# Head scores by blocks of 32 and 64, and reordered steps at the group changes of a hybrid Fourier / HGRN2 diffusion step

## The reference, cut to what matters

```python
def trunk_layer(x, cond, w_mod, b_mod, norm_pre, norm_post, ffn_w_in, ffn_w_out, ...):
    mod = (jax.nn.silu(cond) @ w_mod + b_mod)[:, None, :]
    sh1, sc1, g1, sh2, sc2, g2, sh3, sc3, g3 = jnp.split(mod, N_MOD, axis=-1)
    h = rms_norm(x, norm_pre[0]) * (1.0 + sc1) + sh1
    x = x + 0.5 * g1 * rms_norm(swiglu(h, ffn_w_in[0], ffn_w_out[0]), norm_post[0])
    h = rms_norm(x, norm_pre[1]) * (1.0 + sc2) + sh2
    m, s_f, s_b = mixer(h, w_in, w_four, hgrn_gain, w_hgrn, w_out, lb, s0_f, s0_b, rows)
    x = x + g2 * rms_norm(m, norm_post[1])
    h = rms_norm(x, norm_pre[2]) * (1.0 + sc3) + sh3
    x = x + 0.5 * g3 * rms_norm(swiglu(h, ffn_w_in[1], ffn_w_out[1]), norm_post[2])
```

## Time and profile before

| what | value |
|---|---|
| median of 3 runs | 1507.5 (1505.93 to 1507.74) |
| profiled execution, its own time | 1505.78 |
| its span | 1504.0 |
| PE busy | 1455.7 (97%), 9059 matmul instructions |
| PEld busy | 1342.7 (89%) |
| DVE, ACT, POOL busy | 423.7, 485.4, 615.1 |
| DMA, share of 16 engines (queue q1) | 36.3% |
| mean granted TensorE clock | 0.994 |

### The profile page before, as it was taken

How to read it: one execution, slowest core, us unless ns; L and a number is a source line. 1 busy time by engine, 2 the same in 40 slices (tenths; PEclk the granted TensorE clock), 3 DMA queues, 4 the chain that set the end, 5 groups by cost and what they waited for, 6 DMA issues and landing times.

```text
span 1504.0 us, 21142 instructions
## 1 busy us (share of the span) xinstructions
PE 1455.7 (97%) x9059; PEld 1342.7 (89%) x9059; DVE 423.7 (28%) x616; ACT 485.4 (32%) x666; POOL 615.1 (41%) x486
## 2 busy tenths in 40 slices
PE   3999999999999999999999999999999999999997
PEld 2889989999887878999999999988999999998876
DVE  3311111211001431387777322135211111110042
ACT  5312122222233553233443322266212222232233
POOL 1333333344566663232222334543223343356664
PEclk9999999999999999999999999999999999999999
DMA  9576554222545551211111222323122222235454
GB/s 324 184 234 215 182 190 160 71 83 73 164 128 154 166 205 43 60 46 46 50 50 47 71 71 84 122 75 85 43 71 71 71 85 71 71 103 160 129 183 167
DMA packets 215137, 173.19 MB, mean 115 GB/s; under 512 B 6456, under 2 KB 175620, under 8 KB 214916
## 3 DMA queue, kind: packets, MB, share of 16 engines
q1 hardware_dynamic: 212676, 170.78, 36.3%
q10 hardware_dynamic: 2368, 1.07, 0.2%
HBM read 168.65 MB, written 3.17 MB: 114 GB/s over the span
## 4 chain that ended last, share of the span: by engine, by line
PE 90%; DVE 4%; ACT 3%; issue 1%; POOL 1%; DMA 1%; SPq 0%; DVEq 0%; ACTq 0%
PE PP L496 59%; PE PP L515 7%; PE PP L517 7%; PE PP L516 7%; PE PP L793 2%; PE PP L554 2%; PE PP L690 1%; PE PP L540 1%; DVE XTOK L1483 1%; POOL W_lo L461 1%; DMA W_in<-in_ffn_w_out 1%; DVE YB L1471 1%; DVE W_lo L1509 1%; PE PP L809 1%; ACT W_hi L998 0%
## 5 line engine op out<-in xcount | busy, mean ns | idle before, releaser
L461 POOL TENSOR_TENSOR W_lo<-W_in,W_hi 128x512 fp32r<-128x512 f32 (+1 forms) x452 | 575.0, 1297 | 873.6 <-ACT W_hi L998 873.2
L998 ACT ACTIVATE W_hi<-W_in 128x1024 fp32r<-128x1024 f32 x217 | 229.4, 1058 | 672.4 <-PE PP L496 468.9
L496 PE MATMUL PP<-Hhi,W_hi 128*128 128x320 f32 (+1 forms) x1792 | 417.8, 312 | 0.0
L496 PE MATMUL PP<-Hhi,W_lo 128*128 128x320 f32 (+1 forms) x1792 | 412.0, 309 | 0.0
L496 PE MATMUL PP<-Hlo,W_hi 128*128 128x320 f32 (+1 forms) x1792 | 411.9, 309 | 0.0
L496 PEld LDWEIGHTS PP<-Hhi,W_hi 128*128 128x128 f32 x1792 | 299.1, 188 | 12.9 <-issue 12.7
L496 PEld LDWEIGHTS PP<-Hlo,W_hi 128*128 128x128 f32 x1792 | 300.9, 188 | 0.0
L496 PEld LDWEIGHTS PP<-Hhi,W_lo 128*128 128x128 f32 x1792 | 300.5, 188 | 0.0
L515 PE MATMUL PP<-W_hi,Mhi 128*128 128x512 f32 x440 | 173.3, 394 | 6.8 <-DVE W_lo L1509 4.9
L517 PE MATMUL PP<-W_hi,Mlo 128*128 128x512 f32 x440 | 171.9, 391 | 0.0
L516 PE MATMUL PP<-W_lo,Mhi 128*128 128x512 f32 x440 | 171.9, 391 | 0.0
(11 more groups left out here) (213 smaller groups left out, 1367.6 us busy)
## 6 DMA issues: line engine op xcount, KB each, us to landing
W_in<-in_ffn_w_out SPq DMA_DIRECT2D x176, 256.0 KB, 3.4
W_in<-in_ffn_w_in SPq DMA_DIRECT2D x83, 512.0 KB, 3.8
modl<-in_w_mod SPq DMA_DIRECT2D x14, 2048.0 KB, 9.5
W_in<-in_w_in SPq DMA_DIRECT2D x32, 512.0 KB, 3.8
modw<-in_w_mod SPq DMA_DIRECT2D x4, 2048.0 KB, 13.8
HL<-g_rows SPq DMA_DIRECT2D x6, 512.0 KB, 5.9
V_in<-in_w_in SPq DMA_DIRECT2D x10, 256.0 KB, 5.1
O_in<-in_w_out SPq DMA_DIRECT2D x10, 256.0 KB, 5.5
```

The costliest lines, as they stand in the source:

```text
L461: return nc.gpsimd.tensor_tensor(lo[:, k0:k1, :], full[:, k0:k1, :], hi[:, k0:k1, :].bitcast(fp32), ALU.subtract)
L496: m = mm(out[:, 0:c1 - c0], w[:, k, :], src[:, c0:c1], start=lead and n == 0 and a == 0, stop=tail and n == len(x) - 1 and a == 2)
L998: A(W[i][0], W[i][2], ACT.Copy).then_inc(hi_done, 1)
```

## The change

1. **Head scores.** The diagonal and levels 1 to 6 are made in blocks of 32 x 32 (20 matmuls of 32 columns in place of 5 of 128; for each tile four, one on each 32-column group of the array), level 7 in blocks of 64 x 64 (10 matmuls). Levels 1 to 5 are merged under a mask of 32 columns into a small tile `ATN`; level 6 copies `ATN` and its own blocks into `AT` with eight copies, level 7 with two.
2. **Start.** GpSimd takes (2, 0) third and waits before it until four k slices of the first tokens are ready; ScalarE makes the second high part before the modulation row.
3. **First output, second group.** VectorE makes slab 3's low part between the gains of block 0 and block 1, and slab 20's goes to GpSimd. The first slabs of the value stage alternate between kept buffers and the ring, with other release points.
4. **Mixer's output.** ScalarE takes tile 3's second square and `y_std` before tile 2's `h_high_half`, which comes before `x_square` of tile 3; `h_hi` of tile 2 comes after `x_hat` of tile 3. VectorE follows.
5. **Second output.** Slab 3's low part is moved as in 3. The last three slabs run by token tile (`last_slabs`), tile 3 first; the last tile's add and store are made in two halves.

```diff
-    ("vuA", 8, [1, 2, 0] + KEEP, False), ("vuB", 8, [1, 2, 0] + KEEP, True),
+    ("vuA", 8, [6, 1, 7, 2, 8, 0, 9, 10], False), ("vuB", 8, [6, 1, 7, 2, 8, 0, 9, 10], True),
...
-    for n, k in enumerate((11, 14, 17, 21, 21)):
-        free[base["vuA"] + 3 + n] = base["out0B"] + half + k // 2
+    for n, k in ((0, 11), (2, 14), (4, 17), (6, 21), (7, 21)):
+        free[base["vuA"] + n] = base["out0B"] + half + k // 2
...
-    FIRST_LO = [(0, 0), (1, 0), (0, 1), (1, 1), (2, 0), (2, 1)]
-    LO_DVE = [BASE["out0B"] + m for m in (3, 7, 10, 13, 17, 20)]
+    FIRST_LO = [(0, 0), (1, 0), (2, 0), (0, 1), (1, 1), (2, 1)]
+    LO_DVE = [BASE["out0B"] + m for m in (3, 7, 10, 13, 17)]
...
+            if (i, half) == (2, 0):
+                pool.wait_ge(sem("h0_ready"), KT // 2)
...
+        def last_slabs():
+
+            n = out_slabs(2)
+            for t in GROUP[1]:
+                for m in range(2 * n - LAST, 2 * n):
+                    wide(BASE["out1B"] + m, Mhi, Mlo, 2 * (m % n), (t,), lambda t: y_bank(2, t, 1), False,
+                         m == 2 * n - 1, "y_done" if t == 3 else None, t == 4)
...
             for ch in range(NCH):
-                cols = tile_cols(ch)
-                m = mm(flat(pair_of(hd, 0))[:, cols], KX[0][:, cols], QD[:, 0, hd % 2, cols], start=True, stop=True)
+                for q in range(4):
+                    at = ch * P + 32 * q
+                    m = mm(near(pair_of(hd, 0))[32 * q:32 * q + 32, ch, :], KX[0][:, at:at + 32],
+                           QD[:, 0, hd % 2, at:at + 32], start=True, stop=True)
...
-                m = mm(flat(pair_of(hd, lev))[:, tile_cols(ch)], KX[lev % 2][:, tile_cols(ch)],
-                       level_ap(QD, hd, ch * P, P, 1 << (lev - 1)), start=True, stop=True)
+                if lev == 7:
+                    for q in range(2):
+                        at, other = ch * P + 64 * q, ch * P + 64 * (1 - q)
+                        m = mm(far(pair_of(hd, lev))[64 * q:64 * q + 64, ch, :], KX[lev % 2][:, at:at + 64],
+                               QD[:, 1 - q, hd % 2, other:other + 64], start=True, stop=True)
+                    continue
+                for q in range(4):
+                    at, other = ch * P + 32 * q, ch * P + 32 * (q ^ 1)
+                    queries = QD[:, (q ^ 1) % 2, hd % 2, other:other + 32] if lev == 6 else \
+                        level_ap(QD, hd, at, 32, 1 << (lev - 1))
+                    m = mm(near(pair_of(hd, lev))[32 * q:32 * q + 32, ch, :], KX[lev % 2][:, at:at + 32],
+                           queries, start=True, stop=True)
...
             y_square(1, 3, 0)
-            h_high_half(1, 2)
-            h_hi(1, 2)
             y_square(1, 3, 1)
             y_std(1, 3)
+            h_high_half(1, 2)
             x_square(1, 3)
             x_hat(1, 3)
+            h_hi(1, 2)
...
-            for blk in range(2):
-                for t in GROUP[0]:
-                    y_gain(b, t, blk)
+            for t in GROUP[0]:
+                y_gain(b, t, 0)
+            slab_low(OUT_B[b], 3)
+            for t in GROUP[0]:
+                y_gain(b, t, 1)
...
+            if lev <= NEAR:
+                V.copy_predicated(ATN[:, :, :], near_mask[:, lev - 1:lev, :].to_broadcast([P, NCH, 32]),
+                                  near(pair_of(hd, lev))).then_inc(sem("at_done"), 1)
+            elif lev == 6:
+                for q in range(4):
+                    part, other = slice(32 * q, 32 * q + 32), slice(32 * (q ^ 1), 32 * (q ^ 1) + 32)
+                    V.tensor_copy(tiles[part, :, part], ATN[part, :, :])
+                    m = V.tensor_copy(tiles[part, :, other], near(pair_of(hd, lev))[part, :, :])
+                m.then_inc(sem("at_done"), 1)
```

More of the change, by code:

```diff
@@ L65 @@
 HB = 33
+NEAR = 5
 NLAT = 8 * HB
@@ L215, in hybrid_step_kernel @@
     OSQ = place("OSQ", [P, T], fp32, at=tile_at(27))
+    ATN = place("ATN", [P, NCH, 32], fp32, at=tile_at(27))
     KTOK = place("KTOK", [P, 8, P], fp32, at=tile_at(28))
@@ L449, in _ @@
         load_out(2, 1, wo1)
-        for t in range(NCH):
+        for t in range(NCH - 1):
             sp.wait_ge(sem("x_new"), 2 * NCH + t + 1)
@@ L454, in _ @@
             sp.dma_start(dst, XTOK[:, t, :]).then_inc(sem("y_out"), 16)
-        sp.wait_ge(sem("y_out"), 16 * NCH)
+        for half in range(2):
+            cols = slice(half * WIDE, half * WIDE + WIDE)
+            sp.wait_ge(sem("x_last"), half + 1)
+            sp.dma_start(y_sample[0, 3 * P:4 * P, cols], XTOK[:, 4, cols]).then_inc(sem("y_out"), 16)
+        sp.wait_ge(sem("y_out"), 16 * (NCH + 1))
     @block.gpsimd
@@ L1098, in out_group @@
                 root_table(1 + b)
-            for m in range(2 * n):
+            for m in range(2 * n if (b, grp) != (2, 1) else 2 * n - LAST):
                 after_slab(i + m, 2 if grp else 1)
@@ L1109, in out_group @@
                 y_square(b, t, 1)
+                if (b, grp) == (2, 1):
+                    y_std(b, t)
         def first_steps(b, m):
@@ L1382, in _ @@
         out_group(2, 1)
-        y_std(2, 3)
-        y_std(2, 4)
     @block.vector
@@ L1484, in x_add, with x_add_last @@
                                    quads(XTOK[:, t, :]), ALU.mult, ALU.add).then_inc(sem("x_new"), 1)
+        def x_add_last():
+            dve.wait_ge(sem("y_sd"), 3 * NCH)
+            link(V.reciprocal(ST[:, 4, 4:5], ST[:, 3, 4:5]))
+            dve.wait_ge(sem("y_g"), y_seq(2, 4, 1) + 1)
+            for half in range(2):
+                ks, cols = slice(4 * half, 4 * half + 4), slice(half * WIDE, half * WIDE + WIDE)
+                V.scalar_tensor_tensor(quads(XTOK[:, 4, cols]), YB[:, ks, tile_cols(4)], ST[:, 4, 4:5],
+                                       quads(XTOK[:, 4, cols]), ALU.mult, ALU.add).then_inc(sem("x_last"), 1)
         def x_scale(b, t):
@@ L1540, in first_group @@
             else:
-                y_sum(2, 0)
-                slab_low("out1B", 3)
-                x_add(2, 0)
-                for t in (1, 2):
+                for t in GROUP[0]:
                     y_sum(2, t)
@@ L1552, in first_group @@
                     slab_low("out1B", m)
-            for t in GROUP[1]:
-                y_gain(b, t, 1)
-            y_sum(b, 3)
-            y_sum(b, 4)
-            x_add(b, 3)
-            x_add(b, 4)
+            if b == 0:
+                for t in GROUP[1]:
+                    y_gain(b, t, 1)
+                for t in GROUP[1]:
+                    y_sum(b, t)
+                for t in GROUP[1]:
+                    x_add(b, t)
+            else:
+                y_gain(2, 3, 1)
+                y_sum(2, 3)
+                x_add(2, 3)
+                y_sum(2, 4)
+                y_gain(2, 4, 1)
+                x_add_last()
         def hidden(n, j, c0, c1, u):
@@ L1810, in _ @@
                 y_gain(1, t, 0)
-                h_affine(1, t - 1)
-                h_low(1, t - 1)
+            if t == 4:
+                h_affine(1, 3)
+                h_low(1, 3)
             y_gain(1, t, 1)
```

34 lines of the change are left out of this document (24 added, 10 removed).

## The result

The changed kernel takes 1480.37 us in the median (1479.52 to 1483.41), the kernel before 1506.72 (1505.62 to 1507.74), four runs each: a ratio of 0.983, 95% interval 0.981 to 0.985. The forecast was 1483.7, from 1474 to 1496. The profiled execution took 1479.52 with a span of 1477.7, so the span fell by 26.3 where my sum had 23.8.

What follows compares the result with a forecast made beforehand. TensorE, carrying 90% of the span, was taken to bound the kernel. Head scores 11.3 and the other parts 12.5 summed to 23.8 us, from 1505.78 to 1482.0 profiled, 1483.7 for the median of the runs; range 1474 to 1496.

Steps and rivals of the forecast that it cites:

- head scores: Diagonal and levels 1 to 7 in small blocks on column groups: 11.3 us gained (4.3 to 15.6).
- start: GpSimd held off before the first FFN matmul: 2.41 us less what the clock takes back, taken as 2.0.
- (a): First FFN output, slab 3's low part ahead of the gains: its wait goes, net 3.1 us (1.5 to 4.2).
- (b): First FFN output, slab 20 from VectorE to GpSimd: the wait of 1.73 goes, 1.9 us gained (1.0 to 1.9).
- (c): Value slabs start in a buffer free earlier: two waits for GpSimd go, 2.2 us gained (1.0 to 2.3).
- mixer's output: Tile 3's second square and y_std go earlier: TensorE's wait for the normalised tile goes, 2.5 us (1 to 2.7).
- slab 3, second output: Second FFN output, moved low part delays y_sum, slab 4's high part and GpSimd: 0.6 us lost (-1.2 to +0.4).
- end: Second output's tail: 2.6 us gained behind the last matmul, less a new 1.2 wait for slab 21, net 1.4.
- if that cover were gone, level 6's copies would cost a head at most the 0.87: Head scores: copies lie beside a 3.5 us slab quarter; without it, at most one whole copy's 0.87 us a head.
- The step on level 6: Three of four heads: VectorE's chain from the next head's gate stays, so the wait before level 6 grows to near 0.9.
- 1.7 or 2.4 us: Visit times of two rivals: instructions one after another, 1510 us, chance 0.07; hand-over bound, 1527 us, chance 0.04.
- Waits come back: Rival: new orders give back most removed waits, parts 2 to 5 bring 5 not 12.5, time 1491; chance 0.09.

Runs made afterwards that it cites:

- after: The changed kernel with all five parts, against the kernel before: 1480.37 us in the median, ratio 0.983.
- the run without the heads: The changed kernel with the head scores of before (whole 128 by 128 tiles), all other parts kept: 1495.22 us, ratio 0.992 against the kernel before.

## Why the prediction was right

By its own steps, spans of the two profiled executions, gains in us:

| step | forecast | in the two traces | and in the runs |
|---|---|---|---|
| head scores | 11.3 | 11.1 | alone 12.7 |
| start | 2.0 | 0.65 | 1.2 on the mean of the traces |
| (a) slab 3, first output | 3.1 | 4.0 | 1.8 without the lower clock |
| (b) slab 20 | 1.9 | 2.0 | (b) and (c) together |
| (c) value slabs | 2.2 | 2.5 | 3.8 to 4.7 |
| mixer's output | 2.5 | 2.0 | not undone alone |
| slab 3, second output | -0.6 | 2.1 | not told apart from 0 |
| end | 1.4 | 1.9 | 2.6, with another 1.7 of waits in its trace |
| sum | 23.8 | 26.3 | |

The sum came out nearer than its terms: in these two traces the forecast of the start was 1.3 too high and that of slab 3 in the second output 2.7 too low, and the latter is a matter of the execution. That part of the agreement is luck.

**Head scores.** The mechanism held and the total hides two misses that cancel. A visit was forecast at 0.75 and costs 0.69, because a round costs 0.034 and not 0.040; diagonal and level 1 together save 1.48 a head without their wait, where I had 1.17. Some 3 us more were saved than in my sum. Against it stand the step "if that cover were gone, level 6's copies would cost a head at most the 0.87": I priced eight small copies at one large one. They took 2.5 us, the cover was gone, and three heads wait 0.8 more before the key values; another 0.3 to 0.5 a head went before level 1 (second head: 1.60 from the start of the product ahead of it, 1.32 before). Taking four of the copies off VectorE removed the wait. The step on level 6 was right: its wait was forecast near 0.9 and the delay grew from 0.72 to 1.14.

**Start.** VectorE's chain fell to 3.38 us (31.81 to 35.19), as forecast, though it began 0.4 later than before, so the first matmul came at 35.19 and not near 34.8. The term that was mis-sized is the clock: of my two cases, 2.41 (the clock rises as long after the start) and 1.2 (at the same moment), the lower came out on the mean, and I had taken a value nearer to the upper. In after's own trace it rose later than either, 0.8 us behind before's, and 0.65 was left.

**First output.** (a) Both sizes were off: the new wait at slab 4 (0.9) did not come, since the moved 1.23 us begin at 478.39, while VectorE would stand idle for the first square, and the first sum comes 3.07 after the start of the first square (before: 2.94); instead GpSimd, beside that same subtraction, was late one slab earlier, 0.93 where it had been 0.47. (b) and (c) were right to 0.3, but I missed what GpSimd's full queue does to VectorE: its sums of one column end some 2 us late in six of the nine traces with this part and two-input sums, which costs nothing, and 9.7 us late in three, which costs 2.4 to 3.9 us. The 1483.41 at the top of after's spread may be such an execution; there is no trace of it.

**Mixer's output.** The 2.67 of delay went, and 0.27 remain before the transposes, with 0.16 at the start of the stage.

**Second output.** The loss of 0.6 for slab 3 was wrong: its 1.23 us begin at 1413.44, before ScalarE's first square is done, so most of it lies in a wait of VectorE, and the sum comes 3.1 us after the start of the first square where it came 2.9 before. The 2.1 us gained came with the earliest landings of a load, where VectorE was ahead of GpSimd by 0.03 us. No run has the old place with a landing as early, so whether the move itself has any part in it is open. The new place has a cost that I did not see: behind GpSimd's half the low part takes up to 2.28.

**End.** The new wait (1.18 and restart) is the forecast one. The path from the last matmul's start to the end shrank by 3.2, from 9.1 to 5.9, not by 2.6.

The rivals: no visit is near 1.7 or 2.4 us, so instructions on four column groups do run at once (40 in 0.49 us, 12 ns each). The rule of the Trainium skill's page TensorEngine Tiling, section Instruction Overhead, gave 1.35 us a visit by an estimate from its figure; the trace does not agree, with 0.69. "Waits come back" happened in part: 2.4 before the key values, 1.3 at slab 21, at times 2.4 to 3.9 for the hold, against a forecast of 12.5 and a measured 15.2 outside the heads.

## What to carry to other kernels

A small matmul on column groups costs a fixed price of entering and leaving plus a small one per round: measure both by doubling the rounds before deciding how finely to cut. When an engine's copies are cut into pieces, price them one by one and ask who is queued behind them. Before an engine's queue is filled so that it never pauses, look for short instructions of its neighbour that need a pause. When two engines hold each other up, look at which is due first and by how much, because here 0.03 us decided it. And read a gain or loss of 2 us from several executions, not from one trace.

## What was not expected of the hardware

**VectorE can be held through several of GpSimd's instructions.** A sum of one column a partition (two inputs) takes 0.15 us alone, 2.36 for two beside GpSimd in after, and 9.80 in the run without the heads, ending 0.08 us after GpSimd's fourth slab since the sums began. Two inputs decide: with one input it took 0.33 for two, and the next instruction with two inputs took 8.56. The Trainium skill has this lock (SBUF - State Buffer, section on the two separate sides): the pair is held exclusively, by whichever of the two starts first, for the whole instruction, and on VectorE's side an instruction with two inputs in SBUF counts. The traces agree on who is held, and on who comes first deciding (slab 3 of the second output: 1.23 on VectorE and 3.62 on GpSimd where VectorE was first, 2.28 and 2.55 where GpSimd was), and show that the wait can last not one instruction but eight, until the other engine runs out of work. It need not: in after GpSimd does not pause either, and VectorE gets its turn where one slab ends (545.5). Why it is sometimes one slab and sometimes four is open.

**The lower clock is no certain cost of a wait.** After waits of 2.2 to 2.6 us in the first output it came in three of six traces, and at the start it ended anywhere between 38.2 and 41.2 us.
